# A decoder block's expert activation: three VectorE operations a half, an earlier second half, and regions in another order

## The reference

```python
gu = xc @ w_gate_up[e] + b_gate_up[e]
g, u = gu[:, :D_EXPERT], gu[:, D_EXPERT:]
g = jnp.minimum(g, SWIGLU_LIMIT)                      # 7.0
u = jnp.clip(u, -SWIGLU_LIMIT, SWIGLU_LIMIT)
act = (u + 1.0) * (g * jax.nn.sigmoid(SWIGLU_ALPHA * g))   # 1.702
return act @ w_down[e] + b_down[e]
```

## Time and profile before

| | |
|---|---|
| median of 3 runs | 2152.6 us (2151.63 to 2152.64) |
| the profiled execution | 2151.84 us |
| its span | 2150.2 us |
| granted TensorE clock, mean | 0.973 |
| TensorE busy | 2004.9 us (93%) |
| VectorE busy | 1598.8 us (74%) |
| ScalarE busy | 1293.9 us (60%) |
| GpSimd busy | 290.8 us (14%) |
| moved by DMA | 489.57 MB, 228 GB/s over the span |

### The profile page before, as it was taken

The page is one execution under the profiler, slowest core; times in us unless marked ns, Lnnn a source line. Parts: engine busy times, 40 slices in busy tenths (PEclk is TensorE's granted clock), DMA queues, the critical chain, the costliest instruction groups (busy, mean ns, idle before and its releaser), DMA issues.

```text
span 2150.2 us, 37083 instructions
## 1 busy us (share of the span) xinstructions
PE 2004.9 (93%) x11768; PEld 1532.1 (71%) x11769; DVE 1598.8 (74%) x2100; ACT 1293.9 (60%) x1755; POOL 290.8 (14%) x334
## 2 busy tenths in 40 slices
PE   6999899999898399999999999999999999999993
PEld 5777677777687277777777777777777777777772
DVE  4778755545655488797877779977878988977894
ACT  5555454444533267676665667766667767755774
POOL 3100000000124201111112111121101101210100
PEclk9999999999998699999999999999999999999996
DMA  5020111010634769798888889978889979878994
GB/s 175 20 98 1 40 40 40 20 39 1 215 133 140 170 219 378 279 341 313 286 291 291 283 290 380 375 264 286 287 290 377 376 260 375 311 258 285 377 339 165
DMA packets 256003, 489.57 MB, mean 228 GB/s; under 512 B 20043, under 2 KB 38311, under 8 KB 255856
## 3 DMA queue, kind: packets, MB, share of 16 engines
q1 hardware_dynamic: 233824, 439.56, 57.2%
q0 software_dynamic: 21088, 49.35, 8.7%
q10 hardware_dynamic: 1040, 0.00, 0.0%
HBM read 461.01 MB, written 32.05 MB: 229 GB/s over the span
## 4 chain that ended last, share of the span: by engine, by line
PE 80%; DVE 7%; issue 4%; ACT 4%; DMA 2%; SPq 1%; POOL 0%; ACTq 0%; DVEq 0%; POOLq 0%
PE psum L749 15%; PE psum L750 14%; PE psum L753 14%; PE psum L766 8%; PE psum L455 3%; PE psum L585 3%; PE psum L589 3%; PE psum L587 3%; PE psum L457 2%; PE psum L456 2%; PE psum L737 2%; PE psum L692 1%; PE psum L716 1%; DVE o_lo L1490 1%; PE psum L693 1%
## 5 line engine op out<-in xcount | busy, mean ns | idle before, releaser
L1679 DVE TENSOR_TENSOR w_lo<-ring,w_hi 128x1024 fp32r<-128x1024 f32 x768 | 914.9, 1221 | 142.8 <-ACT w_hi L1056 131.5
L1056 ACT ACTIVATE w_hi<-ring 128x1024 fp32r<-128x1024 f32 x768 | 803.6, 1059 | 275.1 <-PE psum L753 265.9
L749 PE MATMUL psum<-w_hi,rows_hi 128*128 128x512 f32 x1024 | 422.1, 412 | 4.2 <-DVE rows_lo L1683 2.5
L750 PE MATMUL psum<-w_hi,rows_lo 128*128 128x512 f32 x1024 | 399.9, 391 | 0.0
L753 PE MATMUL psum<-w_lo,rows_hi 128*128 128x512 f32 x1024 | 316.2, 390 | 0.0
L749 PEld LDWEIGHTS psum<-w_hi,rows_hi 128*128 128x128 f32 x1024 | 193.8, 189 | 46.7 <-issue 10.3
L753 PEld LDWEIGHTS psum<-w_lo,rows_hi 128*128 128x128 f32 x1024 | 192.5, 188 | 41.1
L750 PEld LDWEIGHTS psum<-w_hi,rows_lo 128*128 128x128 f32 x1024 | 193.2, 189 | 37.5
L749 PE MATMUL psum<-w_hi,act_hi 128*128 128x512 f32 x512 | 219.8, 429 | 0.0
L750 PE MATMUL psum<-w_hi,act_lo 128*128 128x512 f32 x512 | 202.8, 396 | 0.0
L766 PE MATMUL psum<-ring,region_m 128*32 128x256 f32 x3072 | 174.2, 380 | 0.0
(11 more groups left out here) (333 smaller groups left out, 2997.7 us busy)
## 6 DMA issues: line engine op xcount, KB each, us to landing
ring<-in_w_gate_up_dram SPq DMA_DIRECT2D x128, 2048.0 KB, 16.1
ring<-in_w_down_dram SPq DMA_DIRECT2D x64, 2048.0 KB, 14.1
ring<-in_w_in_dram SPq DMA_DIRECT2D x16, 512.0 KB, 5.2
region_m<-in_x_dram SPq DMA_DIRECT2D x8, 512.0 KB, 11.6
ring<-in_w_in_dram SPq DMA_DIRECT2D x2, 2048.0 KB, 17.5
ring<-in_w_out_dram SPq DMA_DIRECT2D x2, 2048.0 KB, 7.5
region_a<-in_x_dram POOLq DMA_DIRECT2D x8, 512.0 KB, 4.8
acc_rows<-region_a POOLq DMA_DIRECT2D x8, 512.0 KB, 3.3
```

The lines of the kernel that those rows point to most:

```text
L749: mm(bank(i), hi[:, ks], wh, start=(k0 + q == 0), stop=False)
L750: mm(bank(i), lo[:, ks], wh, start=False, stop=False)
L1056: act.activation(w_hi[:, n % NBUF, :], place[i][:, k0 * HALF:(k0 + 2) * HALF], ACT.Copy).then_inc(hi_done, 1)
L1679: v.tensor_tensor(out=w_lo[:, n % NBUF, :], in0=place[i][:, k0 * HALF:(k0 + 2) * HALF], in1=w_hi[:, n % NBUF, :].bitcast(f32), op=ALU.subt ...
```

## The change

- The 1 of (u + 1) is added to the up half of the bias before it is split, in one more VectorE operation in `bias_part(0)`. The up values are then limited to -6 and 8.
- The gate part of a half is one product, the gate in PSUM times its sigmoid. The limit moves behind it: g x sigmoid(1.702 g) is limited to its value at 7, in the same operation that multiplies with the up values. So a half takes three operations where it took four, and one wait among them less. The tail's activation is changed in the same way.
- The sigmoid of half 1 stands behind high part 13 in ScalarE's queue where it stood behind high part 16, `gate_part(1)` behind low part 13 in VectorE's where it stood behind 17, and `up_part(1)` behind 17 where it stood behind 18. The gate product has a tile for each half.
- region_m is placed behind region_s and region_a instead of ahead of them.

```diff
-SIG_LIMIT = 1.0 / (1.0 + math.exp(-LIMIT * ALPHA))
+GLU_LIMIT = LIMIT / (1.0 + math.exp(-LIMIT * ALPHA))
...
-        at_m = next_base()
-        region_m = sb("region_m", [P, LM * (SEQ + 3) + LM * SEQ])
         at_s = next_base()
         region_s = sb("region_s", [P, LM * SEQ])
         at_a = next_base()
         region_a = sb("region_a", [P, A_COLS])
+        at_m = next_base()
+        region_m = sb("region_m", [P, LM * (SEQ + 3) + LM * SEQ])
...
-        glu = take(HALF)
+        glu = [take(HALF) for _ in range(2)]
...
                             if n == 8:
                                 sigmoid(0)
+                            if n == 13:
+                                sigmoid(1)
                             if n == 16:
                                 actT_out(0)
-                                sigmoid(1)
...
                     dve.wait_ge(bias_in, 96)
+                    then(v.tensor_scalar(bstage[0:96, D:2 * D], bstage[0:96, D:2 * D], 1.0, None, ALU.add))
                     then(v.tensor_copy(bias3[0:96, :], bstage[0:96, :]))
...
                         def gate_part(half):
                             dve.wait_ge(gsig_done, j * 2 + half + 1)
-                            v.tensor_scalar(gsig[half], gsig[half], SIG_LIMIT, None, ALU.min).then_inc(glu_step, 1)
-                            dve.wait_ge(glu_step, j * 6 + 3 * half + 1)
-                            v.scalar_tensor_tensor(out=glu, in0=bank(2 * half), scalar=LIMIT, in1=gsig[half],
-                                                   op0=ALU.min, op1=ALU.mult).then_inc(glu_step, 1)
+                            v.tensor_tensor(out=glu[half], in0=bank(2 * half), in1=gsig[half], op=ALU.mult).then_inc(glu_step, 1)
 
                         def up_part(half):
                             dve.wait_ge(unit_mm[2 * half + 1], j + 1)
-                            v.tensor_scalar(act_rows[half], bank(2 * half + 1), LIMIT, -LIMIT, ALU.min, ALU.max).then_inc(glu_step, 1)
-                            dve.wait_ge(glu_step, j * 6 + 3 * half + 3)
-                            v.scalar_tensor_tensor(out=act_rows[half], in0=act_rows[half], scalar=1.0, in1=glu,
-                                                   op0=ALU.add, op1=ALU.mult).then_inc(act_done, 1)
+                            v.tensor_scalar(act_rows[half], bank(2 * half + 1), LIMIT + 1.0, 1.0 - LIMIT, ALU.min, ALU.max).then_inc(glu_step, 1)
+                            dve.wait_ge(glu_step, j * 4 + 2 * half + 2)
+                            v.scalar_tensor_tensor(out=act_rows[half], in0=glu[half], scalar=GLU_LIMIT, in1=act_rows[half],
+                                                   op0=ALU.min, op1=ALU.mult).then_inc(act_done, 1)
...
                             if n == 11:
                                 up_part(0)
+                            if n == 13:
+                                gate_part(1)
                             if n == 16:
                                 actT_low(0)
                             if n == 17:
-                                gate_part(1)
-                            if n == 18:
                                 up_part(1)
```

More of the change, by code:

```diff
@@ L1711, in tail_glu_part @@
+                            dve.wait_ge(glu_step, j * 4 + 2 * half + 2)
+                            v.scalar_tensor_tensor(out=act_rows[half], in0=glu[half], scalar=GLU_LIMIT, in1=act_rows[half],
+                                                   op0=ALU.min, op1=ALU.mult).then_inc(act_done, 1)
                         def tail_glu_part():
                             wait_reg(dve, tgsig_done, before + 1)
-                            v.tensor_scalar(tail_sig, tail_sig, SIG_LIMIT, None, ALU.min).then_inc(tglu_step, 1)
@@ L1714, in tail_glu_part @@
-                            wait_reg(dve, tglu_step, before * 3 + 1)
-                            v.scalar_tensor_tensor(out=tail_glu, in0=bank(1)[:, 0:QC], scalar=LIMIT, in1=tail_sig,
-                                                   op0=ALU.min, op1=ALU.mult).then_inc(tglu_step, 1)
+                            v.tensor_tensor(out=tail_glu, in0=bank(1)[:, 0:QC], in1=tail_sig, op=ALU.mult).then_inc(tglu_step, 1)
                             wait_reg(dve, tup_mm, before + 2)
-                            v.tensor_scalar(tail_act, bank(0)[:, 0:QC], LIMIT, -LIMIT, ALU.min, ALU.max).then_inc(tglu_step, 1)
@@ L1719, in tail_glu_part @@
-                            wait_reg(dve, tglu_step, before * 3 + 3)
-                            v.scalar_tensor_tensor(out=tail_act, in0=tail_act, scalar=1.0, in1=tail_glu,
-                                                   op0=ALU.add, op1=ALU.mult).then_inc(tact_done, 1)
+                            v.tensor_scalar(tail_act, bank(0)[:, 0:QC], LIMIT + 1.0, 1.0 - LIMIT, ALU.min, ALU.max).then_inc(tglu_step, 1)
+                            wait_reg(dve, tglu_step, before * 2 + 2)
+                            v.scalar_tensor_tensor(out=tail_act, in0=tail_glu, scalar=GLU_LIMIT, in1=tail_act,
+                                                   op0=ALU.min, op1=ALU.mult).then_inc(tact_done, 1)
```

## The result

The changed kernel takes 2138.2 us (median of 4 runs, 2137.4 to 2140.1) where the kernel before takes 2152.6 (4 runs, 2151.6 to 2153.7): a ratio of 0.9934, 95% interval 0.9917 to 0.9951. That is 14.4 us less, beyond the 0.2% that a measurement can tell. The forecast was 24.0 less, 2127.8, with a range of 2118 to 2143: the sign and the range hold, the size was too large by 10 us.

What follows compares the result with a forecast made beforehand. TensorE's own pace and its holes were taken to bound the expert loop and output projection. Terms -14.4 + 3.2 - 10.2 - 2.6 = -24.0 from 2151.8 gave 2127.8 us, range 2118 to 2143.

Steps and rivals of the forecast that it cites:

- The first hole: Half 1's transposes (L777) wait for VectorE's last activation operation in 16 steps without a tail: 0.90 us each, 11.7 idle together.
- (a): Three VectorE operations per half instead of four: some 0.45 us saved per half, counting only through (b); tail part 0.
- (b): Half 1's sigmoid and gate part sooner in the queues: hole before half 1's transposes gone, -14.4 us; piece 16 costs +3.2.
- the tie at piece 16: Low part of half 0 lands just as TensorE's weight load wants it: 0.2 us a step, +3.2 us (0 to +8).
- (c): All three regions start on multiples of 128 bytes: act pieces -10.2 us, output projection -2.6; at least nothing.
- (d): Adding 1 to the bias, one more VectorE operation in the router loop: hidden in 5.07 us of idle time, 0.
- (e): Weight transfers when steps grow 1.0 to 1.2 us shorter: 6.6 us in hand, hidden, 0.
- Rival 1: TensorE's pace does not follow the address, so only the queue-order terms count: 2140.6 us; chance 0.17.
- rival 2: Slow pace follows a region's place, not alignment, so rows pieces and gates slow down: +2.7, 2154.5 us; chance 0.07.
- Rival 3: The wait at piece 16 takes back the whole hole, 0.9 us x 16; alignment works: 2139.0 us; chance 0.08.
- Rival 4: The new queue order fails; the last activation operation stays late by the old amount: 2139.0 us; chance 0.05.
- rival 5: After piece 16's wait, the jump over tail code needs a DMA fetch, 5.1 us x 16: 2206.2 us; chance 0.05.

## Why the prediction was right or wrong

**What bounds the kernel** held: TensorE's pace and its holes. The first hole was read right in place, count and size.

**(a)** The saving of 0.45 us on VectorE was right (37.16 to 36.71 in the old order). That it "counts through (b)" was not: (b) makes VectorE wait for the sigmoid, and there it is worth 0.13.

**(b)** The layout of the two queues was right almost to the hundredth: ScalarE's wait of 1.9 us (1.89), the tie at piece 16, the last activation operation in time, the hole of L777 gone. Two things failed. The first is "I take 0.2 us, near the middle" for the tie: a tie with a test behind it costs what the test costs, the upper bound of the row, 0.5 us from the low part's end to the load, of which 0.33 are lost. The second is larger and was not a number but an omission: "What is late next is piece 16" ends the search there. Piece 20 has such a pair of wait and test as well. Set against the bias product ahead of piece 16, TensorE was ready for it 0.72 us sooner (the last pair of piece 19 behind it by 6.05 us, before 6.77), and the low part of half 1 only 0.32 sooner (its end behind it by 6.43, before 6.75)., read for the price of the test, already showed it with nothing in hand: the load followed 0.54 us after the low part. The difference, 0.40, was lost. Together 0.73 per step where +0.2 was taken: 11.7 us against 3.2, which is 8.5 of the 10 us.

**(c)** The mechanism was right in kind, its rule wrong: "multiples of 128 bytes" would have made the kernel with 64 bytes of padding fast. What the runs show is the start modulo 256 relative to the other operand. Before, region_s and region_a stood 64 bytes off the ring's residue; 128 off is slow as well. The size was too large: -12.8 forecast; the new order of regions alone gave 7 us by the ratio. The projection gave 2.1 of its 2.6. A step gains 0.20 and not 0.32. The 0.04 was read by setting the act piece right behind the transposes (1345.75 to 1347.15) against a rows piece in the middle of a unit; the rows piece behind the transposes takes 1.38 (1332.05 to 1333.43), not 1.36. The act pieces come in pairs with transposes or a bias product between them, and only the second of a pair gains as much as 0.04. The first gains 0.02, as pieces 20 and 21 show, from first product to first product, before and after:

```profile
1345.43 0.48 PE L749 MATMUL psum<-w_hi,act_hi 128*128 128x512 f32 x1
...
1346.92 0.39 PE L749 MATMUL psum<-w_hi,act_hi 128*128 128x512 f32 x1
...
1348.32 0.39 PE L737 MATMUL psum<-region_s,region_m 96*128 96x512 bf16 x1
```

```profile
1336.63 0.48 PE L749 MATMUL psum<-w_hi,act_hi 128*128 128x512 f32 x1
...
1338.10 0.39 PE L749 MATMUL psum<-w_hi,act_hi 128*128 128x512 f32 x1
...
1339.46 0.39 PE L737 MATMUL psum<-region_s,region_m 96*128 96x512 bf16 x1
```

With the regions alone in the new order, pieces ahead of L777 gave nothing either, since the wait there is VectorE's. The Trainium skill's page "TensorE: Matmul & The Clock Gate", section "Wait — 56ns, not 53.3ns?", lets the start-to-start time of the bf16 products that it measured follow from the column count alone, at a given clock. The traces here don't agree for fp32r: at clock 1.00 its products have two paces at 512 columns, 0.227 and 0.233 us, and 128 bytes more of padding switch between them. So siding with the row was right.

**(d), (e)** The added operation ran at 598.99 for 0.68 us, and VectorE was still idle 4.06 us behind it: 0 was right. No transfer of weights became a wait of ScalarE, VectorE or TensorE, even at 36.0 us a step.

**The rivals.** Rival 1 (the address has no part) and rival 2 (the place) are refuted by the padded kernels. Rival 3 named the right place and gave it the wrong size; what it describes, the whole gain of 0.9 taken back at piece 16, is 0.33 there and 0.73 once piece 20 is counted. Its 2139.0 lies closest to the 2138.2 measured, but by luck: it gives the alignment 12.8 us, which gave 8.5 (16 steps of each kind at 0.20, and 2.1), and the order nothing, which gave 3.7 (16 x 0.23). Rival 4 has the same number and is refuted: the last activation operation ends at 1331.23, 0.90 us ahead of the transposes that need it, and L777 waits no more. For the jump over the tail code, rival 5, there is no fetch to be seen: the delay behind the late wait is 0.51 us at piece 16, where code is jumped over, and 0.54 at piece 20, where it is run.

**The number.** The gain that is shown to be the change's is 12.3 us, half of the 24.0 forecast. That 2138.2 lies in the range is owed to rival 1, for which the range was drawn out to 2143; the bounds of the sum's own terms end at 2138. With +11.7 in place of +3.2 the sum would have been 2136.3, and with the measured gains of the act pieces, the projection and the hole it comes to about 2140; the other 2 us are in no term of it.

## What to carry to other kernels

When a wait is removed or shortened by moving work in a queue, follow the faster engine through every later wait of the same step, not just the next one, and lay the new arrival against each; a wait in hand by less than the time gained is the next hole. Keep waits as late as the data allow, behind tests, jumps and work that doesn't need them: in this loop moving two waits gave 0.86 us a step, while the new order of two engines, as written, cost 0.15 (36.71 to 36.86). Whether moved waits would give as much in the old order was not tried. And for fp32r products like these, place the tiles that TensorE reads together at equal starts modulo 256 bytes.

## What the runs showed of the hardware

- A 512-column fp32r product takes 0.227 us from start to start when its loaded and its streamed tile start equally modulo 256 bytes, 0.233 when they differ by 64 (the kernel before) or 128 (the run with 64 bytes of padding, and the regions 128 bytes further). These are the paces inside a run of pieces, 1.36 and 1.40 us for six; the first piece behind a bias product or transposes differs by 0.03 or less between the two. Moving all tiles together by 128 changes nothing.
- A wait on TensorE that is met late and is followed by a test delays the next weight load: it came 0.51 us after the producer's end at piece 16, 0.54 at piece 20. With no test between, it was 0.05 us (L777, 1341.17 to 1341.22 before), and 0.13 at piece 16 with the wait behind the test. When the wait is met before TensorE gets there, the same test costs nothing that the trace shows (piece 16 with half 1 behind piece 14). Whether the delay is the test itself, the read of its register or, at piece 20, the second wait was not tried apart; a jump over code is not needed for it, as piece 20 shows.
- It was not tried which of the two tiles, loaded or streamed, suffers from unequal starts, nor in what steps below 64 bytes. Of the projection's products L693 loads from region_m, which starts equally with the ring, and was as slow (median 397 ns before, 389 after) as L692, which loads from region_s; so by these durations a product's pace hangs on its neighbours' tiles as well.
